# First low-rank products of an RWKV-7 layer on column tiles of the matmul array, and one value mix moved ahead of a low part

## The reference, cut to what matters

```python
xx = token_shift(x) - x
xs = x[None] + xx[None] * mix[:, None, None, :]
rkv = jnp.einsum('nbtc,ncd->nbtd', xs[:3], w_rkv)
r, k, v = rkv[0], rkv[1], rkv[2]
xw, xa, xg = xs[3], xs[4], xs[5]
w = -jax.nn.softplus(-(w0 + jnp.tanh(xw @ w1) @ w2)) - 0.5    # decay, w1: 1024 x 64
a = jax.nn.sigmoid(a0 + (xa @ a1) @ a2)                       # rate,  a1: 1024 x 64
g = jax.nn.sigmoid(xg @ g1) @ g2                              # gate,  g1: 1024 x 160
kk = heads(k * k_k)
```

## Time and profile before

| | us |
|---|---|
| three timed runs | 686.83, 688.43, 689.33 |
| median | 688.43 |
| profiled execution, first to last instruction (span) | 686.9 |

### The profile page before, as it was taken

One profiled execution on the slowest core, in us unless ns is written; L12 is line 12 of the kernel. 1 busy time (PEld: TensorE's weight loads), 2 busy tenths in 40 slices (PEclk: granted clock), 3 DMA queues, 4 the chain that ended last, 5 costly groups with the idle time before them and its releaser, 6 DMA issues. The chain is left out here.

```text
span 686.9 us, 13967 instructions
## 1 busy us (share of the span) xinstructions
PE 629.0 (92%) x6047; PEld 432.9 (63%) x6047; DVE 363.6 (53%) x585; ACT 262.6 (38%) x384; POOL 96.8 (14%) x128
## 2 busy tenths in 40 slices
PE   4999979989989879899999989999979989999994
PEld 4775857868868767544444359997757754444432
DVE  4894987834566586412323476587644641233236
ACT  5464642443253424231112345566643432112112
POOL 6970055040033030000000000012120000000000
PEclk9999989999999999999999999999999999999998
DMA  8952442200000138999999732543301999999911
GB/s 314 275 199 66 149 157 89 101 4 5 4 4 5 63 142 320 410 409 409 410 408 409 297 126 84 164 135 128 105 1 64 411 408 409 409 410 409 408 72 63
DMA packets 48643, 145.16 MB, mean 211 GB/s; under 512 B 4808, under 2 KB 4976, under 8 KB 48576
## 3 DMA queue, kind: packets, MB, share of 16 engines
q1 hardware_dynamic: 47696, 142.28, 54.9%
q0 software_dynamic: 880, 1.91, 1.0%
HBM read 143.11 MB, written 1.05 MB: 210 GB/s over the span
## 5 line engine op out<-in xcount | busy, mean ns | idle before, releaser
L1169 DVE TENSOR_TENSOR w_lo<-w_ring,w_hi 128x2048 fp32r<-128x2048 f32 x32 | 75.6, 2369 | 22.0 <-PE ps L1863 11.9
L708 ACT ACTIVATE w_hi<-w_ring 128x2048 fp32r<-128x2048 f32 x32 | 60.8, 1909 | 53.4 <-PE ps L1863 30.6
L1861 PE MATMUL ps<-w_hi,xa_hi 128*128 128x512 f32 x128 | 53.3, 417 | 11.6 <-issue 5.2
L1356 DVE SCALAR_TENSOR_TENSOR hact_s<-silu_s,slot_gates,ps 128x256 f32<-128x256 f32 x16 | 7.7, 480 | 104.8 <-issue 76.5
L1862 PE MATMUL ps<-w_lo,xa_hi 128*128 128x512 f32 x128 | 52.1, 407 | 0.0
L1863 PE MATMUL ps<-w_hi,xa_lo 128*128 128x512 f32 x128 | 52.0, 406 | 0.0
L679 POOL TENSOR_TENSOR att<-att,causal 128x256 f32<-128x256 f32 x16 | 14.9, 950 | 257.9 <-ACT att L1105 257.9
L2402 PE MATMUL ps<-load,xe 128*64 128x512 f32 x192 | 43.3, 597 | 4.2 <-ACT xe L813 2.6
L2415 PE MATMUL ps<-load,hs 128*64 128x512 f32 x192 | 43.3, 593 | 0.5 <-DVE y_lo L1362 0.4
L2402 PE MATMUL ps<-load,xT 128*64 128x512 f32 x192 | 43.7, 608 | 0.0
L822 ACT ACTIVATE silu_s<-ps,slot_gates 128x256 f32<-128x256 f32 x16 | 7.6, 472 | 91.9 <-issue 81.3
(11 more groups left out here) (369 smaller groups left out, 1407.6 us busy)
## 6 DMA issues: line engine op xcount, KB each, us to landing
load<-in_moe_w_gate_dram SPq DMA_DIRECT2D x48, 512.0 KB, 11.7
load<-in_moe_w_up_dram SPq DMA_DIRECT2D x48, 512.0 KB, 12.8
load<-in_moe_w_down_dram SPq DMA_DIRECT2D x48, 512.0 KB, 14.0
w_ring<-in_rw_w_rkv_dram SPq DMA_DIRECT2D x24, 512.0 KB, 6.5
w_ring<-in_moe_w_gate_dram SPq DMA_DIRECT2D x16, 512.0 KB, 12.2
w_ring<-in_moe_w_up_dram SPq DMA_DIRECT2D x16, 512.0 KB, 13.3
w_ring<-in_moe_w_down_dram SPq DMA_DIRECT2D x16, 512.0 KB, 12.0
w_ring<-in_w_kv_dram SPq DMA_DIRECT2D x16, 512.0 KB, 5.1
```

The lines of the kernel that those rows point to most:

```text
L708: nc.scalar.activation(whi[n % HI][:, :, :], w_ring[n % RING][:, :, :], ACT.Copy).then_inc(hi_ready, 1)
L1169: nc.vector.tensor_tensor(wlo[n % LO][:, :, :], w_ring[n % RING][:, :, :], whi[n % HI][:, :, :].bitcast(f32), ALU.subtract).then_inc(lo_re ...
L1861: nc.tensor.matmul(dst, xh, wh, start=start, stop=False)
```

## The change

Decay and rate are multiplied in turns: a block of decay on the array's columns 0 to 63, a block of rate on columns 64 to 127, so that the two results stand in partitions 0 to 63 of bank 4 and 64 to 127 of bank 5. The gate's last 32 channels are split by block over four tiles of 32 columns, two blocks on each; the four partial sums are copied by ACT to `g_parts` and added by one product with `add_tiles`, a matrix of stacked identities that the router already uses. That product stands between the halves of the `w2x` products. On DVE, `mix_v` moves ahead of `xb_lo`, and `xa_lo` behind `kk`.

```diff
-                nc.scalar.activation(za[0:LW, :], PS[0:LW, 5, 0:T], ACT.Copy).then_inc(rw["z"], 1)
+                nc.scalar.activation(za[0:LW, :], PS[LW:2 * LW, 5, 0:T], ACT.Copy).then_inc(rw["z"], 1)
                 act.wait_ge(rw["lora1"], 3)
+                nc.scalar.activation(g_parts[:, :], PS[:, 7, 0:T], ACT.Copy).then_inc(rw["g_parts"], 1)
                 nc.scalar.activation(zg[:, :], PS[:, 6, 0:T], ACT.Sigmoid).then_inc(rw["z"], 1)
-                nc.scalar.activation(zg2[:, :], PS[0:LG - P, 7, 0:T], ACT.Sigmoid).then_inc(rw["z"], 1)
+                act.wait_ge(rw["lora1"], 4)
+                nc.scalar.activation(zg2[:, :], PS[0:LG - P, 7, T:2 * T], ACT.Sigmoid).then_inc(rw["z"], 1)
                 x_hi(4, xb_hi, 1)
...
                 mix(4)
-                x_lo(4, xb_hi, xb_lo, 1)
                 dve.wait_ge(rw["lora1"], 2)
                 mix(5)
-                x_lo(5, xa_hi, xa_lo, 2)
+                x_lo(4, xb_hi, xb_lo, 1)
...
                                             ).then_inc(rw["kk0"], 1)
+                x_lo(5, xa_hi, xa_lo, 2)
                 split_next(4)
...
-                for i, (bank, c0, n) in enumerate(((4, 0, LW), (5, LW, LW), (6, 2 * LW, P), (7, 2 * LW + P, LG - P))):
-                    pe.wait_ge(rw["mixed"], min(i, 2) + 5)
...
-                    for b in range(NC):
-                        mm = nc.tensor.matmul(PS[0:n, bank, 0:T], lora1[:, b, c0:c0 + n], src[:, b, :],
+                pe.wait_ge(rw["hn_act"], 4)
+                pe.wait_ge(rw["mixed"], 6)
+                for b in range(NC):
+                    for i in range(2):
+                        o = slice(i * LW, (i + 1) * LW)
+                        mm = nc.tensor.matmul(PS[o, 4 + i, 0:T], lora1[:, b, o], mixed_[1 + i][:, b, :],
                                               start=b == 0, stop=b == NC - 1)
-                    if i != 2:
-                        mm.then_inc(rw["lora1"], 1)
+                        if b == NC - 1:
+                            mm.then_inc(rw["lora1"], 1)
+                pe.wait_ge(rw["mixed"], 7)
+                for b in range(NC):
+                    nc.tensor.matmul(PS[:, 6, 0:T], lora1[:, b, 2 * LW:2 * LW + P], mixed_[3][:, b, :],
+                                     start=b == 0, stop=b == NC - 1)
+                for b in range(NC):
+                    mm = nc.tensor.matmul(PS[b % 4 * LT:(b % 4 + 1) * LT, 7, 0:T], lora1[:, b, 2 * LW + P:2 * LW + LG],
+                                          mixed_[3][:, b, :], start=b < 4, stop=b >= 4)
+                mm.then_inc(rw["lora1"], 1)
...
+                        if i + j == 0:
+                            pe.wait_ge(rw["masks"], 1)
+                            pe.wait_ge(rw["g_parts"], 1)
+                            nc.tensor.matmul(PS[0:LG - P, 7, T:2 * T], add_tiles[:, :], g_parts[:, :],
+                                             start=True, stop=True).then_inc(rw["lora1"], 1)
                     mm.then_inc(rw["lora2"], 1)
```

More of the change, by code:

```diff
@@ L276, in trunk_program @@
         zg2 = rplace("zg2", [LG - P, T], 107)
+        g_parts = rplace("g_parts", [P, T], 107)
         kk_row = place("kk_row", [P, C], at=h_at)
@@ L389, in trunk_program @@
                 rw = {q: sem(f"rw_{q}") for q in
-                      ("hn_act", "lora_loaded", "rows_loaded", "late_loaded", "x_again",
+                      ("hn_act", "g_parts", "lora_loaded", "rows_loaded", "late_loaded", "x_again",
                        "mixed", "x_hi", "x_lo", "lora1", "z", "lora2", "sig", "a", "k", "r", "v",
@@ L1897, in rwkv_phase @@
                 pe.wait_ge(rw["lora_loaded"], 16 * 7)
-                for i, (bank, c0, n) in enumerate(((4, 0, LW), (5, LW, LW), (6, 2 * LW, P), (7, 2 * LW + P, LG - P))):
-                    pe.wait_ge(rw["mixed"], min(i, 2) + 5)
-                    if i == 0:
-                        pe.wait_ge(rw["hn_act"], 4)
-                    src = mixed_[1 + min(i, 2)]
-                    for b in range(NC):
-                        mm = nc.tensor.matmul(PS[0:n, bank, 0:T], lora1[:, b, c0:c0 + n], src[:, b, :],
-                                              start=b == 0, stop=b == NC - 1)
-                    if i != 2:
-                        mm.then_inc(rw["lora1"], 1)
+                pe.wait_ge(rw["hn_act"], 4)
[4 more added lines that the diff above has]
+                        mm = nc.tensor.matmul(PS[o, 4 + i, 0:T], lora1[:, b, o], mixed_[1 + i][:, b, :],
+                                              start=b == 0, stop=b == NC - 1)
+                        if b == NC - 1:
[8 more added lines that the diff above has]
+                mm.then_inc(rw["lora1"], 1)
+                pe.wait_ge(rw["z"], 1)
+                pe.wait_ge(rw["k"], 2)
                 for i, (zz, w2) in enumerate(((zw, w2x), (za, a2x))):
[L1909 to L1912, removed]
+                    if i == 1:
                         pe.wait_ge(rw["z"], 4)
```

## The result

The changed kernel takes 682.14 us as the median of 4 runs (679.15 to 683.11), against 688.13 for the kernel before (686.83 to 689.33, 4 runs): a ratio of 0.990 with a 95% interval of 0.987 to 0.993, or 6.0 us. Forecast were 678.3, with a range of 676.0 to 683.2: faster as said, inside the range, with 6 us gained where 10 were forecast. In every run the time lies about 1.7 us above the span.

What follows compares the result with a forecast made beforehand. PE bounds the first low-rank products, DVE the stretch from 70.78 to 98.20. 7.2 us at piece 9 plus 2.9 of clock give 10.1 off the 686.9 span: 676.8, median 678.3, range 676.0 to 683.2.

Steps and rivals of the forecast that it cites:

- Decay beside rate: First low-rank products on PE: decay and rate together take what one group takes now, 3.55 us.
- The gate on four tiles: Gate's last 32 channels on PE: 1.00 us on four tiles against 3.57 on one.
- The add: Adding product between the halves of `w2x`: two records and two changes of columns, 0.65 to 0.85 us, taken as 0.8.
- Piece 4: PE reaches piece 4 at 57.84 instead of 63.11, 5.27 us earlier.
- The rule on weight loads: Column-tile products on PE: by the rule 16 pairs need 5.6 us, by the trace 3.5; the forecast followed the trace.
- Waits for `g_parts`, `zg2`, `sig`, `xb_lo`: PE up to piece 4 waits for none of these; covers 1.3, 1.4, 0.8 and 1.5 us.
- DVE's part: `w_lo` of piece 6 starts 7.23 us earlier: 5.27 by PE, 1.95 because `kk` no longer stands ahead.
- Piece 9: Starts when its `w_lo` is ready, at 91.2 instead of 98.43; PE waits 2.3 us instead of 3.32.
- The clock behind that wait: Behind the wait ahead of piece 9 granted clock stays at 1.00, saving a further 2.9 us.
- rival 1: Clock falls again behind the shorter wait at piece 9; only 7.2 us saved, 681.2; chance 0.36.
- Rivals 2, 3 and 5: Weight loads not hidden, 683.6, chance 0.04; tiles run one after another, 687.3, 0.04; each turn drains the array, 697, 0.03.
- rival 4: DVE's chain is held by something else, piece 9 starts at 98.43 as now: 688.4; chance 0.03.

Runs made afterwards that it cites:

- joint_only: Kernel before with decay and rate in turns on two column halves alone; gate's products and DVE's order as before: 684.52 us, ratio 0.9923.
- gate_only: Kernel before with the gate's last 32 channels on four tiles and the adding product alone: 688.26 us, ratio 0.9991.
- dve_only: Kernel before with DVE's two reorderings alone, PE's products as before: 687.49 us, ratio 0.9986.
- pe_only: Changed kernel with DVE's order put back as before: 682.88 us, ratio 0.9914.
- the second profile: Profile of the changed kernel run again unaltered: 682.88 us, ratio 0.9905 to the kernel before.
- the filler ahead of piece 9: Small unused products in PE's wait: 13 in the kernel before, 685.21 us, ratio 0.9939; 10 in the changed kernel, 678.83 us, ratio 0.9844.
- blocked: Changed kernel with all eight decay products before all eight of rate, same column halves, not in turns: 684.15 us, one run.

## Why the prediction was right, and where not

- *What bounds:* right up to piece 9. PE's stretch was PE's alone, and from piece 6 on DVE set the pace.
- *Decay beside rate:* 3.55 forecast, 3.61 measured. *The gate on four tiles:* 1.00 and 1.00. *The add:* 0.8 and 0.74. *Piece 4:* 5.27 earlier, forecast and measured; split into 3.45 and 1.82 by `joint_only` and `gate_only`.
- *The rule on weight loads:* the Trainium skill (TensorE: Matmul & The Clock Gate, The mechanism) lets a load overlap running products only in another row group. Refuted here: sixteen pairs in 3.61 us, on all rows, with loads of 0.137 and a pair every 0.215, leave no room for that.
- *Waits for `g_parts`, `zg2`, `sig`, `xb_lo`:* none, as forecast.
- *DVE's part:* 7.23 forecast for `w_lo` of piece 6, 7.20 measured; at piece 9 1.93 of this are the two reorderings (`dve_only`) and 5.26 the products (`pe_only`).
- *Piece 9:* 7.2 earlier, as forecast; the wait ahead of it is 2.56 where I had 2.3, since piece 8 began and ended a little earlier still (6.44 against 6.2). With 2.56 the comparison by which I chose the clock comes out even: 0.76 from the 3.32 with a drop, 0.76 from the 1.80 without.
- *The clock behind that wait:* this is the step that failed, as "I take it that the clock stays up and the 2.9 us are saved too", together with the sum that let the gain last to the end ("PE's work and that chain move together"). The price was right (2.86 and 2.87). But behind the same wait the clock stayed up in one profile of the changed kernel and fell in the other, for half as long as in the profile of before; and what was kept there was lost again at `in_chunk`, around the first router and near the last experts, where the clock falls in some runs for 3.4 us, in others for 6.8, in others not at all. I had taken these places from one profile of before as fixed. My own sign of being wrong, "a stage behind piece 11 gives the time back", came true in part: 4.92 of 10.06 us in one profile, 6.26 of 8.42 in the other. The median gained 6.0; that this is the 7.2 that don't depend on the clock, less what later low clock takes, fits but isn't shown, since the profiles themselves end 5.14 and 2.16 earlier.
- *The time:* 682.14 lies 3.8 over the forecast. That it lies in the range owes nothing to the clock term: the range was made to hold rival 1 as well. Rival 1 (7.2 saved, 681.2) was the closer forecast. Rivals 2, 3 and 5 are refuted by `joint_only` and the pair rows, rival 4 by the start of piece 9.

Open: what makes the chunks at clock 1.00 take 0.5 us more (2.6 in the second profile); why the clock falls at a place in one run and not in the next; and whether the filler ahead of piece 9 brings more than the 2.9 that piece 9 loses (4.2 by both pairs of ratios, which the intervals don't tell from 2.9).

## What to carry to other kernels

Products that use few output columns can share the array when they are issued in turns on different columns; a chain on another engine must then be shortened with them (here by moving one product into an idle place), or it keeps part of the gain. Where the engine's clock falls behind a wait, price that fall apart from the wait, and don't book it as gained unless something holds the clock: the same wait ended in either way. With runs that differ by 9 us, read single terms from stage starts, which agreed to 0.01 us between two profiles up to the first place where the clock differed (and not behind it), and only the whole from many runs.

## Not expected of the hardware

- Half clock lasted 6.8 us while PE was busy without a gap (6.80 of 6.80, 33 records) at the last `in_chunk` products, of 2 moving columns each, and the small products and transposes behind them; PE had been busy without a gap ahead of the fall too (6.56 of 6.56 from 107.24 on). Seven further products of 128 moving columns among them did not prevent it in three profiles of four.
- Across column tiles products did not start in program order: in `blocked` a rate record started at 43.90, ahead of decay records that stand before it in the program and started at 44.11 to 44.54. The order of the code on PE is thus not always the order of the starts.
